# The delta rule's diagonal blocks, transposed and masked where they lie

## The chip, the cores and the metric

The kernel runs on one core of a Trainium2 chip. The metric is the device time of one execution in microseconds. The core has TensorE for matrix products, VectorE, ScalarE and GpSimd for elementwise work, and DMA queues for transfers. SBUF is the on-chip memory with 128 partitions; PSUM is where TensorE's products go.

## What is computed

One block of a network on a sequence of 512 rows of 2048 numbers, with three branches: a gated delta rule with 8 heads, an S5 state layer and a cross-attention to a memory. Their outputs are gated, summed and projected. The change lies in the delta rule. For each head and chunk it solves a triangular system, `eye + lower`:

```
def chunked_gated_delta_rule(q, k, v, g, beta):
    ...
    lower = jnp.where(strict, jnp.einsum('bnhid,bnhjd->bnhij', k_beta, k) * decay, 0.0)
    eye = jnp.eye(CHUNK, dtype=q.dtype)
    rhs = jnp.concatenate([v * beta[..., None], k_beta * jnp.exp(gc)[..., None]], axis=-1)
    sol = lax.linalg.triangular_solve(eye + lower, rhs, left_side=True, lower=True, unit_diagonal=True)
    u_val, w_dec = sol[..., :dv], sol[..., dv:]
    ...
```

## The kernel before

All large projections are written as products of float32 numbers split in a high and a low part: ScalarE makes `wh` of a weight block (line 508), VectorE makes `wl`, the rest (line 516), and TensorE runs three products for each pair of tiles (lines 522 to 524). A weight block comes in two halves of 128x1024, with two slots of each tile, and TensorE waits on semaphore `w_lo` before each half.

In the mixer stage the projections for head i+1 run on TensorE while the delta rule and the S5 groups of head i are worked on by the other engines. There are ten weight blocks per head, of eight portions each; the small products of the delta rule and of S5 are put between the portions. The order is written out by hand, for TensorE in one `mixer` function and for VectorE in another: each engine has one queue and goes through it in order, with semaphores between the engines.

The kernel takes chunks of 128 rows, four per head, so `NT` is 4 and `P` is 128. `system` (line 2378) writes the strictly lower matrices of the four chunks into `dl`, 128 partitions by 4 x 128. Their inverse is built from blocks of `B` = 32. `first_blocks` (lines 2385 to 2397) prepares the diagonal blocks: it gathers the sixteen 32x32 blocks into the tile `lb`, with one copy for each quarter of the partitions, transposes them into `lbt`, masks them with `low1` (first neighbours below the diagonal), subtracts the result from the identity in `tb`, and transposes that into `ub`. TensorE then works with `lbt`, `tb` and `ub` in `level_x` and `level_p` (lines 1176 to 1198). On VectorE, `first_blocks` stands behind `keys`, `system` and `values`, and in front of `split(3, 0)`, that is, of the `wl` half that TensorE needs next.

GpSimd has its own queue. In `turn_back` (lines 812 to 815) it multiplies S5's scanned states with cosines and sines, six products of 128x512 per group of states; in `arguments` (lines 791 to 802) it makes the arguments of the tables for a later group.

```
        if j: keys(j); system(j); values(j); first_blocks(j)
        split(3, 0)
        if j: queries(j)
        split(3, 1)
```

Of the kernel before, what the change touches and what calls it, by code (L numbers as in the profile page):

```python
# [21 lines left out]
ALU = mybir.AluOpType  # L22
# [3 lines left out]
P = 128  # L26
# [3 lines left out]
NT = S // P  # L30
# [16 lines left out]
B = 32  # L47
# [42 lines left out]
def count(j, first, per):  # L90

    return j[0] * per + (first + per * j[1])


def wait(e, s, value):

    if isinstance(value, int) and value <= 0:
        return
    e.wait_ge(s, value)


def wait_apart(k, e, s, value):


    wait(e, s, value)
    if not isinstance(value, int):
        e.sem_inc(k.sp_waits if e is k.sp else k.pool_waits if e is k.pool else k.pe_waits, 1)
# [6 lines left out]
def build(nc, x, mem, norm_g, w_in, conv_w, a_log, dt_bias, gdn_g, lam_re, lam_im, log_dt, b_re, b_im,  # L114
          c_re, c_im, s5_d, w_glu, mem_g, w_kv, w_a, w_b, w_c, w_out, final_g, consts, out):
    with ExitStack() as ctx:
        k = Handles()
# [16 lines left out]
        def sb(where, name, shape, dt=F32):  # L134
            return where.enter_context(nc.sbuf_tensor(name, [P] + shape, dt))
# [68 lines left out]
        with ExitStack() as area:  # L204
            k.qraw = sb(area, "qraw", [S + 3])
            k.kraw = sb(area, "kraw", [S + 3])
            k.vraw = sb(area, "vraw", [S + 3])
            k.qc = sb(area, "qc", [S])
            k.kc = sb(area, "kc", [S])
            k.vc = sb(area, "vc", [S])  # L210
            k.zs = sb(area, "zs", [S])
            k.zbs = sb(area, "zbs", [S])
            k.cwh = sb(area, "cwh", [CONV, 3])
            k.braw = sb(area, "braw", [2, 4, GS])
            k.craw = sb(area, "craw", [2, NS])
            k.bpad = sb(area, "bpad", [2, 4, 4, 2, GS])
            k.rq = sb(area, "rq", [S])
            k.zk = sb(area, "zk", [S])
            k.er = sb(area, "er", [NT, P])
            k.qd = sb(area, "qd", [NT, P])  # L220
            k.dl = sb(area, "dl", [NT, P])
            k.du = sb(area, "du", [NT, P])
            k.vb = sb(area, "vb", [NT, P])
            k.kbg = sb(area, "kbg", [NT, P])
            k.kd = sb(area, "kd", [NT, P])
            with ExitStack() as a:
                k.lt = sb(a, "lt", [NT, P])
                k.tl = sb(a, "tl", [NT, P])
            k.sql = sb(area, "sql", [NT, P], F32R)
            k.sqh = sb(area, "sqh", [NT, P], F32R)  # L230
            k.tu = sb(area, "tu", [NT, P])
            k.gx = sb(area, "gx", [NT, P])
            k.lb = sb(area, "lb", [NT, B])
            k.lbt = sb(area, "lbt", [NT, B])
            k.tb = sb(area, "tb", [NT, B])
            k.ub = sb(area, "ub", [NT, B])
            k.xb5 = sb(area, "xb5", [NT, B])
            k.th = sb(area, "th", [NT, 2 * B])
            k.vn = sb(area, "vn", [NT, P])
            k.st = sb(area, "st", [P])  # L240
            k.hph = sb(area, "hph", [4, NT])
            k.hk = sb(area, "hk", [4, NT])
            k.s5h = sb(area, "s5h", [5, 4])
            k.dh = sb(area, "dh", [1])
            k.xb = sb(area, "xb", [S])
            k.bt = sb(area, "bt", [4, 4, GS])
            k.cpad = sb(area, "cpad", [2, 2, NS])
            k.bs = sb(area, "bs", [2, 4, P], F32R)
            k.bc = sb(area, "bc", [2, P])
            k.tcos0 = sb(area, "tcos0", [S])  # L250
            k.tcos1 = sb(area, "tcos1", [S])
            k.tsin0 = sb(area, "tsin0", [S])
            k.tsin1 = sb(area, "tsin1", [S])
            k.karg = sb(area, "karg", [S])
            k.farg = sb(area, "farg", [S])
            k.onesr = sb(area, "onesr", [P], F32R)
            k.ma = sb(area, "ma", [S])
            k.mb = sb(area, "mb", [S])
            k.gr = [sb(area, f"gr{q}", [S]) for q in range(4)]
            with ExitStack() as a:  # L260
                k.gi0 = sb(a, "gi0", [S])
                k.gi1 = sb(a, "gi1", [S])
                k.hr = [sb(a, f"hr{q}", [S]) for q in range(4)]
            with ExitStack() as a:
                k.xbh = sb(a, "xbh", [S], F32R)
                k.xbl = sb(a, "xbl", [S], F32R)
                k.x4 = sb(a, "x4", [4, S], F32R)
# [722 lines left out]
def tensor_program(k, pe):  # L990
# [185 lines left out]
    def level_x(j, l):  # L1176

        if l == 1:
            wait_apart(k, pe, k.tu_s, count(j, 7, 8))
            wait_apart(k, pe, k.qkt, count(j, 1, 1))  # L1180
        else:
            wait_apart(k, pe, k.tus, count(j, 2 * l - 3, 17))
        for n in range(NT):
            for r in range(0, P, B):
                mm = pe.matmul(ps[2][r:r + B, n * B:(n + 1) * B], k.lbt[r:r + B, n, :], k.tb[r:r + B, n, :], start=True, stop=True)  # L1185
        mm.then_inc(k.lx, 1)

    def level_p(j, l):

        wait_apart(k, pe, k.xm, count(j, l, 7))  # L1190
        if l == 1:
            wait_apart(k, pe, k.tu_s, count(j, 8, 8))
        else:
            wait_apart(k, pe, k.tus, count(j, 2 * (l - 1), 17))
        for n in range(NT):
            for r in range(0, P, B):
                mm = pe.matmul(ps[6][r:r + B, n * B:(n + 1) * B], k.ub[r:r + B, n, :], k.xb5[r:r + B, n, :], start=True, stop=True)  # L1197
        mm.then_inc(k.lp, 1)
# [108 lines left out]
    def mixer(a, j, l, blocks=PER):  # L1307
# [46 lines left out]
        if j: level_x(j, 1)  # L1354
        until(39)
        if j: level_p(j, 1)
        until(43)
        if j: level_x(j, 2)
# [3 lines left out]
        if j: level_p(j, 2)  # L1362
        until(49)
        if j: level_x(j, 3)
        until(53)
        if j: level_p(j, 3)
# [653 lines left out]
def vector_program(k, dve):  # L2020
    ps, mat, blk, col, stat, tp, hp = k.ps, k.mat, k.blk, k.col, k.stat, k.tp, k.hp
# [8 lines left out]
    tt, ts, stt = dve.tensor_tensor, dve.tensor_scalar, dve.scalar_tensor_tensor  # L2030
# [235 lines left out]
    def rep_chunks(m, n=P):  # L2266
        return m.unsqueeze(1).to_broadcast([P, NT, n])
# [117 lines left out]
    def first_blocks(j):  # L2385

        dve.wait_ge(k.lm, count(j, 1, 1))
        wait(dve, k.lx, count(j, 0, 6))
        for r in range(0, P, B):
            dve.tensor_copy(k.lb[r:r + B, :, :], k.dl[r:r + B, :, r:r + B]).then_inc(k.tu_s, 1)  # L2390
        dve.wait_ge(k.tu_s, count(j, 4, 8))
        dve.transpose(k.lbt[:, :, :], k.lb[:, :, :]).then_inc(k.tu_s, 1)
        tt(k.tb[:, :, :], k.lb[:, :, :], rep_chunks(blk["low1"], B), ALU.mult).then_inc(k.tu_s, 1)
        dve.wait_ge(k.tu_s, count(j, 6, 8))
        tt(k.tb[:, :, :], rep_chunks(blk["ident"], B), k.tb[:, :, :], ALU.subtract).then_inc(k.tu_s, 1)
        dve.wait_ge(k.tu_s, count(j, 7, 8))
        dve.transpose(k.ub[:, :, :], k.tb[:, :, :]).then_inc(k.tu_s, 1)

    def blocked(bank, m=B):
# [94 lines left out]
    def mixer(a, j, l, blocks=PER, heads=True, x=None):  # L2494
# [23 lines left out]
        if j: keys(j); system(j); values(j); first_blocks(j)  # L2518
# [270 lines left out]
```

## Time and profile before

| | |
|---|---|
| median of 3 runs | 2090.88 us (2090.85 to 2091.57) |
| the profiled execution | 2091.08 us |
| its span, first to last instruction | 2089.3 us |
| TensorE busy | 2051.6 us, 98% |
| VectorE busy | 1347.7 us, 65% |
| ScalarE busy | 841.6 us, 40% |
| GpSimd busy | 844.8 us, 40% |

A row of the trace gives the start in us, the duration, the engine (PE is TensorE, DVE VectorE, ACT ScalarE, POOL GpSimd), the line of the kernel, the operation, what it writes and reads, and the shape. An engine's share of busy time alone doesn't tell what bounds the kernel; the waits of the busiest engine do.

### The profile page before, as it was taken

How to read it: one execution, taken by the hardware profiler on the slowest of the kernel's cores; microseconds unless marked ns; L12 is line 12 of the kernel's file. 1: busy time of each engine (PE TensorE's matmuls, PEld its weight loads, DVE VectorE, ACT ScalarE, POOL GpSimd, SP SyncE). 2: the span in 40 equal slices, each digit the busy share in tenths (PEclk: the TensorE clock that was granted, in tenths of full speed). 3: DMA queues.
4: the chain of work that ended last, by engine and by line, in shares of the span. 5: the costliest groups of instructions: out<-in, count | busy, mean ns of one | idle time of the engine just before them, and what ended most of it. 6: DMA issues, size and time to landing. Idle time of an engine off the chain costs nothing.

```text
span 2089.3 us, 32198 instructions
## 1 busy us (share of the span) xinstructions
PE 2051.6 (98%) x12700; PEld 1706.3 (82%) x12700; DVE 1347.7 (65%) x1831; ACT 841.6 (40%) x1113; POOL 844.8 (40%) x631
## 2 busy tenths in 40 slices
PE   7999999999999999999999999999999999999998
PEld 6799888887787877877778777777778888888997
DVE  6554353449789697796977969767443344557766
ACT  5433232354453444434444344363242232223444
POOL 0000000028577586774867848668201100024223
PEclk9999999999999999999999999999999999999999
DMA  9255453455554445555546546455456556455855
GB/s 279 81 156 151 137 171 91 116 131 116 119 123 120 129 113 125 144 133 129 152 126 153 133 126 155 119 144 124 116 161 197 172 153 184 145 147 188 264 174 182
DMA packets 416712, 306.88 MB, mean 147 GB/s; under 512 B 25817, under 2 KB 386626, under 8 KB 415938
## 3 DMA queue, kind: packets, MB, share of 16 engines
q1 hardware_dynamic: 394610, 236.73, 40.8%
q0 software_dynamic: 14736, 55.58, 10.9%
q10 hardware_dynamic: 7232, 12.72, 1.6%
q8 instruction: 92, 1.51, 0.3%
q14 instruction: 42, 0.34, 0.1%
HBM read 269.30 MB, written 60.83 MB: 158 GB/s over the span
## 4 chain that ended last, share of the span: by engine, by line
PE 80%; DVE 11%; ACT 4%; issue 3%; DMA 2%; POOLq 0%; POOL 0%; DVEq 0%; ACTq 0%; SPq 0%
PE bank L522 23%; PE bank L524 22%; PE bank L523 22%; PE bank L1480 2%; PE bank L1483 2%; PE bank L1484 2%; DVE lb L2390 2%; DVE wl L516 1%; DVE tl L2456 1%; DVE gi L2487 1%; PE bank L1304 1%; ACT wh L508 1%; PE bank L1185 1%; PE bank L1197 1%; DMA yst<-s_out 1%
## 5 line engine op out<-in xcount | busy, mean ns | idle before, releaser
L522 PE MATMUL bank<-uh,wh 128*128 128x512 f32 x2176 | 873.0, 401 | 9.4 <-DVE wl L516 6.5
L524 PE MATMUL bank<-uh,wl 128*128 128x512 f32 x2176 | 849.1, 390 | 0.0
L523 PE MATMUL bank<-ul,wh 128*128 128x512 f32 x2176 | 848.9, 390 | 0.0
L516 DVE TENSOR_TENSOR wl<-raw,wh 128x1024 fp32r<-128x1024 f32 x320 | 446.5, 1398 | 382.8 <-ACT wh L508 381.5
L508 ACT ACTIVATE wh<-raw 128x1024 fp32r<-128x1024 f32 x320 | 336.2, 1058 | 470.7 <-DMA raw<-in_w_in_dram 214.5
L522 PEld LDWEIGHTS bank<-uh,wh 128*128 128x128 f32 x2176 | 408.8, 188 | 102.7 <-issue 12.9
L524 PEld LDWEIGHTS bank<-uh,wl 128*128 128x128 f32 x2176 | 408.5, 188 | 88.3
L523 PEld LDWEIGHTS bank<-ul,wh 128*128 128x128 f32 x2176 | 409.2, 188 | 77.3
L771 POOL DMA_DIRECT2D gated_c<-ox x8 | 4.3, 544 | 372.4 <-DVE ox L2153 371.8
L812 POOL TENSOR_TENSOR hr<-tcos,gr 128x512 f32<-128x512 f32 x32 | 52.9, 1654 | 185.4 <-DVE gi L2487 185.4
L909 POOL DMA_DIRECT2D gates<-gates x24 | 17.1, 714 | 199.6 <-DVE merged L2682 127.8
L1702 ACT ACTIVATE gk<-bank 128x512 f32<-128x512 f32 x48 | 28.7, 597 | 164.2 <-PE bank L524 164.2
L522 PE MATMUL bank<-mh,wh 128*128 128x256 f32 x256 | 73.4, 287 | 5.5 <-DVE wl L516 5.5
L524 PE MATMUL bank<-mh,wl 128*128 128x256 f32 x256 | 72.3, 282 | 0.0
L523 PE MATMUL bank<-ml,wh 128*128 128x256 f32 x256 | 72.2, 282 | 0.0
L2615 DVE TENSOR_TENSOR wl<-raw,wh 128x1024 fp32r<-128x1024 f32 x32 | 47.8, 1495 | 31.7 <-ACT wh L1919 31.7
L1480 PE MATMUL bank<-wh,uh 128*128 128x256 f32 x240 | 67.5, 281 | 0.2 <-DVE ul L2598 0.2
L1484 PE MATMUL bank<-wh,ul 128*128 128x256 f32 x240 | 67.3, 281 | 0.0
L791 POOL TENSOR_SCALAR karg<-cst,s5h 128x512 f32<-128x512 f32 x32 | 24.4, 762 | 101.9 <-DVE hph L2274 90.7
L794 POOL TENSOR_SCALAR karg<-karg 128x512 f32<-128x512 f32 x32 | 62.9, 1964 | 0.0
L798 POOL TENSOR_SCALAR karg<-cst,s5h 128x512 f32<-128x512 f32 x32 | 61.3, 1915 | 3.2
L813 POOL TENSOR_TENSOR karg<-tsin,gi 128x512 f32<-128x512 f32 x32 | 62.0, 1938 | 0.0
(410 smaller groups left out, 3355.6 us busy)
## 6 DMA issues: line engine op xcount, KB each, us to landing
raw<-in_w_in_dram SPq DMA_DIRECT2D x224, 512.0 KB, 3.9
raw<-in_w_kv_mem_dram SPq DMA_DIRECT2D x32, 512.0 KB, 3.9
weight_sums<-in_w_out_dram POOLq DMA_DIRECT2D x32, 512.0 KB, 7.6
raw<-weight_sums SPq DMA_DIRECT2D x32, 512.0 KB, 3.8
gates<-gk ACTq DMA_DIRECT2D x48, 256.0 KB, 4.3
gates<-gates POOLq DMA_DIRECT2D x24, 512.0 KB, 4.5
weight_sums<-in_w_out_dram SPq DMA_DIRECT2D x16, 512.0 KB, 5.2
weight_sums<-weight_sums SPq DMA_DIRECT2D x16, 512.0 KB, 5.7
```

What stands on the lines that cost most here:

```text
L508: act.activation(k.wh[slot][:, c], k.raw[slot][:, c], ACT.Copy).then_inc(k.w_hi, 1)
L516: dve.tensor_tensor(k.wl[slot][:, c], k.raw[slot][:, c], k.wh[slot][:, c].bitcast(F32), ALU.subtract).then_inc(k.w_lo, 1)
L522: pe.matmul(o, ah, bh, start=start, stop=False)
L523: pe.matmul(o, ah, bl, start=False, stop=False)
L524: return pe.matmul(o, al, bh, start=False, stop=stop)
L794: ts(k.karg[:, :], k.karg[:, :], -ROUND, None, ALU.add).then_inc(k.args, 1)
L798: ts(k.karg[:, :], k.tvec, lo_, None, ALU.mult).then_inc(k.args, 1)
L812: pool.tensor_tensor(o[:, :], c1[:, :], a[:, :], ALU.mult).then_inc(k.dem, 1)
L813: pool.tensor_tensor(k.karg[:, :], c2[:, :], b[:, :], ALU.mult).then_inc(k.dem, 1)
L1480: mm = pe.matmul(o, hi[:, a], wh, start=t == 0 and i == 0, stop=False)
L1484: mm = pe.matmul(o, lo[:, a], wh, start=False, stop=t == KW - 1 and i == 1)
L2615: tt(k.wyl[n % 4], k.wyr[n % 4], k.wph[n % 2][:, Y_PART, :].bitcast(F32), ALU.subtract).then_inc(k.w_lo, 1)
```

## The change

The tile `lb` is gone. The mask reads the diagonal blocks in `dl` and writes `tb`, in four products of 32 partitions each; the transpose reads them in `dl` and writes `lbt`, in four of 32 partitions. The masks come first, the transposes behind them. The subtraction and the second transpose stay. Semaphore `tu_s` now counts 10 per head and not 8, and the waits on it follow, those of TensorE too.

```
@@ -1176,7 +1175,7 @@
         if l == 1:
-            wait_apart(k, pe, k.tu_s, count(j, 7, 8))
+            wait_apart(k, pe, k.tu_s, count(j, 9, 10))
             wait_apart(k, pe, k.qkt, count(j, 1, 1))
@@ -1189,7 +1188,7 @@
         if l == 1:
-            wait_apart(k, pe, k.tu_s, count(j, 8, 8))
+            wait_apart(k, pe, k.tu_s, count(j, 10, 10))
@@ -2387,13 +2386,12 @@
         dve.wait_ge(k.lm, count(j, 1, 1))
         wait(dve, k.lx, count(j, 0, 6))
         for r in range(0, P, B):
-            dve.tensor_copy(k.lb[r:r + B, :, :], k.dl[r:r + B, :, r:r + B]).then_inc(k.tu_s, 1)
-        dve.wait_ge(k.tu_s, count(j, 4, 8))
-        dve.transpose(k.lbt[:, :, :], k.lb[:, :, :]).then_inc(k.tu_s, 1)
-        tt(k.tb[:, :, :], k.lb[:, :, :], rep_chunks(blk["low1"], B), ALU.mult).then_inc(k.tu_s, 1)
-        dve.wait_ge(k.tu_s, count(j, 6, 8))
+            tt(k.tb[r:r + B, :, :], k.dl[r:r + B, :, r:r + B], rep_chunks(blk["low1"], B)[r:r + B], ALU.mult).then_inc(k.tu_s, 1)
+        for r in range(0, P, B):
+            dve.transpose(k.lbt[r:r + B, :, :], k.dl[r:r + B, :, r:r + B]).then_inc(k.tu_s, 1)
+        dve.wait_ge(k.tu_s, count(j, 4, 10))
         tt(k.tb[:, :, :], rep_chunks(blk["ident"], B), k.tb[:, :, :], ALU.subtract).then_inc(k.tu_s, 1)
-        dve.wait_ge(k.tu_s, count(j, 7, 8))
+        dve.wait_ge(k.tu_s, count(j, 9, 10))
         dve.transpose(k.ub[:, :, :], k.tb[:, :, :]).then_inc(k.tu_s, 1)
```

VectorE's queue in the first head, before, from the values `vb` to the next `wl`:

```order
L2363 TENSOR_TENSOR vb<-bank,hk 128x512
L2390 COPY lb<-dl 32x128 x4
L2392 STREAM_TRANSPOSE lbt<-lb 128x128
L2393 TENSOR_TENSOR tb<-lb,cst 128x128
L2395 TENSOR_TENSOR tb<-cst,tb 128x128
L2397 STREAM_TRANSPOSE ub<-tb 128x128
L516 TENSOR_TENSOR wl<-raw,wh 128x1024
```

And the same stretch of the changed kernel, whose line numbers are one or two lower:

```order
L2362 TENSOR_TENSOR vb<-bank,hk 128x512
L2389 TENSOR_TENSOR tb<-dl,cst 32x128 x4
L2391 STREAM_TRANSPOSE lbt<-dl 32x128 x4
L2393 TENSOR_TENSOR tb<-cst,tb 128x128
L2395 STREAM_TRANSPOSE ub<-tb 128x128
L515 TENSOR_TENSOR wl<-raw,wh 128x1024
```

Eight instructions became ten; what stands before and behind them, and every other engine's queue, is as it was.

## Rows read from the trace of the kernel before

**Rows 1.** The page, busy time of each engine, share of the span, instructions:
```profile
PE 2051.6 (98%) x12700; PEld 1706.3 (82%) x12700; DVE 1347.7 (65%) x1831; ACT 841.6 (40%) x1113; POOL 844.8 (40%) x631
```

**Rows 2.** The page, chain that ended last, share by engine and by line:
```profile
PE 80%; DVE 11%; ACT 4%; issue 3%; DMA 2%; POOLq 0%; POOL 0%; DVEq 0%; ACTq 0%; SPq 0%
PE bank L522 23%; PE bank L524 22%; PE bank L523 22%; PE bank L1480 2%; PE bank L1483 2%; PE bank L1484 2%; DVE lb L2390 2%; DVE wl L516 1%; DVE tl L2456 1%; DVE gi L2487 1%; PE bank L1304 1%; ACT wh L508 1%; PE bank L1185 1%; PE bank L1197
```

**Rows 3.** TensorE in order of time, first and last head, [idle before <-releaser]:
```profile
493.65 0.47 PE L522 MATMUL bank<-uh,wh 128*128 128x512 f32 x1 [0.25 <-DVE wl L516]
...
1417.46 0.47 PE L522 MATMUL bank<-uh,wh 128*128 128x512 f32 x1 [1.57 <-DVE wl L516]
```

**Rows 4.** VectorE in order of time, first head: start us, us, what:
```profile
485.81 0.71 DVE L2390 COPY lb<-dl 32x128 f32<-32x128 f32 x1
486.55 1.34 DVE L2390 COPY lb<-dl 32x128 f32<-32x128 f32 x1
487.92 1.20 DVE L2390 COPY lb<-dl 32x128 f32<-32x128 f32 x1
489.15 1.35 DVE L2390 COPY lb<-dl 32x128 f32<-32x128 f32 x1
490.54 0.31 DVE L2392 STREAM_TRANSPOSE lbt<-lb 128x128 f32<-128x128 f32 x1
490.77 0.58 DVE L2393 TENSOR_TENSOR tb<-lb,cst 128x128 f32<-128x128 f32 x1
491.39 0.67 DVE L2395 TENSOR_TENSOR tb<-cst,tb 128x128 f32<-128x128 f32 x1
492.09 0.32 DVE L2397 STREAM_TRANSPOSE ub<-tb 128x128 f32<-128x128 f32 x1
492.32 1.18 DVE L516 TENSOR_TENSOR wl<-raw,wh 128x1024 fp32r<-128x1024 f32 x1
```

**Rows 5.** GpSimd in order of time, same stretch:
```profile
485.15 1.29 POOL L815 TENSOR_TENSOR hr<-hr,karg 128x512 f32<-128x512 f32 x1
486.52 1.29 POOL L812 TENSOR_TENSOR gr<-tsin,gr 128x512 f32<-128x512 f32 x1
487.77 1.27 POOL L813 TENSOR_TENSOR karg<-tcos,gi 128x512 f32<-128x512 f32 x1
489.12 1.30 POOL L815 TENSOR_TENSOR gr<-gr,karg 128x512 f32<-128x512 f32 x1
490.52 0.69 POOL L791 TENSOR_SCALAR karg<-cst,s5h 128x512 f32<-128x512 f32 x1
491.20 1.59 POOL L792 TENSOR_SCALAR farg<-cst,s5h 128x512 f32<-128x512 f32 x1
```

**Rows 6.** VectorE's instructions by line, count: ns min/median/max, first and last start:
```profile
L2390 DVE COPY lb<-dl x32: 694/1270/1351, 485.8 to 1413.0; 32x128 f32<-32x128 f32 x32
L2416 DVE COPY th<-tb x16: 215/216/218, 542.1 to 1463.4; 32x128 f32<-32x128 f32 x16
L2404 DVE TENSOR_TENSOR xb<-bank,cst x32: 276/290/292, 503.5 to 1455.0; 128x128 f32<-128x128 f32 x32
```

**Rows 7.** The same view, small products with both inputs in SBUF:
```profile
L2360 DVE TENSOR_TENSOR hk<-hk,hph x8: 704/1350/1361, 484.4 to 1408.2; 128x4 f32<-128x4 f32 x8
L2355 DVE TENSOR_TENSOR hk<-hk,hph x8: 162/164/164, 460.4 to 1383.4; 128x4 f32<-128x4 f32 x8
L2292 DVE TENSOR_TENSOR bpad<-bt x32: 221/380/1315, 453.4 to 1372.8; 64x64 f32<-64x64 f32 x32
```

**Rows 8.** VectorE and GpSimd in order of time, near 454 us:
```profile
453.91 1.31 DVE L2292 TENSOR_TENSOR bpad<-bt 64x64 f32<-64x64 f32 x1
...
453.85 1.29 POOL L800 TENSOR_TENSOR farg<-farg,karg 128x512 f32<-128x512 f32 x1
```

**Rows 9.** Transposes of 32 partitions, by line, and four in order of time:
```profile
L2414 DVE STREAM_TRANSPOSE tu<-tb x32: 299/302/307, 540.7 to 1462.8; 32x128 f32<-32x128 f32 x32
...
540.72 1.30 DVE L2414 STREAM_TRANSPOSE tu<-tb 32x128 f32<-32x128 f32 x4
```

**Rows 10.** TensorE in order of time, first products on the diagonal blocks:
```profile
499.29 0.40 PE L1185 MATMUL bank<-tb,lbt 32*32 32x32 f32 x25
```

More of the change, by code:

```diff
@@ L232, in build @@
             k.gx = sb(area, "gx", [NT, P])
-            k.lb = sb(area, "lb", [NT, B])
             k.lbt = sb(area, "lbt", [NT, B])
```

## The prediction

> **What bounds the kernel now.** The profiled execution took 2091.08 us, 0.20 us more than the median of the runs shown, 2090.88; the sum is made on 2091.08 and then carried over to the median. The page's busy table comes first [rows 1]: TensorE is busy for 98% of the span. VectorE is at 65% and GpSimd at 40%. So the end is set by TensorE, and another engine counts only where TensorE waits for it. The chain that ended last [rows 2] gives 80% to TensorE and 11% to VectorE, and names the copies into `lb` (line 2390) with 2%. This invites the thought that the copies' whole time is on the path. The instructions with their idle times correct it: what TensorE stood still for is far smaller.
>
> TensorE's rows in order of time, with the idle time in front of each, have one wait per head at the place of the change, eight in all. The first is 0.25 us, the last 1.57 [rows 3]; the six between are 0.57 to 0.92, and the sum is 5.64 us. Each ends when the first `wl` (line 516) behind the diagonal blocks is there. In the first head VectorE's rows read [rows 4]: four copies 485.81 to 490.50, transpose, mask, subtraction, transpose, then `wl` 492.32 to 493.50; TensorE's next product starts at 493.65 [rows 3]. VectorE has no idle time in between. So whatever is added to or taken from these instructions moves that `wl`, and TensorE has no slack there, in any head. TensorE's next need of VectorE lies later in the same stretch and moves along with TensorE itself.
>
> **Why the copies are slow.** A copy of 32x128 elements between two SBUF tiles takes 215 ns at line 2416, yet these take 694 to 1351 ns [rows 6]. The rows of the four copies against those of GpSimd [rows 4, 5] show why: the copies end at 486.52, 487.89, 489.12 and 490.50, and GpSimd's operations end at 486.44, 487.81, 489.04 and 490.42. Each copy ends 0.08 us behind one of GpSimd's, and GpSimd's next one follows. The two engines take turns, and a copy pays for one GpSimd operation of 1.29 us, four in a row in each head.
>
> **The change part by part, per head.**
>
> 1. The four copies go, and four masked products of the same 32x128 elements take their place, each with two inputs in SBUF. Do they wait for their turn too? The trace has two kinds of small products with both inputs in SBUF to compare with. Line 2360 works on 4 elements per partition, among GpSimd's products, and takes 704 to 1361 ns, where line 2355, the same form elsewhere, takes 162 to 164. Line 2292 changes its first partition from one to the next as the new ones do, and goes from 221 to 1315 ns [rows 7]. One of these runs 453.91 to 455.22 and GpSimd's product 453.85 to 455.14 [rows 8], again a turn. So I take it that the four new products wait for the same four GpSimd operations. What differs is the part behind the wait: line 2393, such a product, ended at 491.35, 0.14 us behind the GpSimd operation that ended at 491.21 [rows 4, 5], the copies 0.08 behind. That is 0.06 us each, and GpSimd starts its next one that much later: 4 x 0.06 = +0.24 us. Bounds: 0, if the product is as quick as a copy, and 4 x 0.08 = 0.32, from the difference of the 292 ns that the product of line 2404 takes at most, on 128x128, and the 215 of line 2416 [rows 6].
>
> 2. The transpose of 128x128 becomes four of 32x128. Line 2414 is four such: 0.30 us each, 1.30 us for the four [rows 9], and with the gap of 0.03 us in front of the next instruction, as between the copies, 1.33. The one that goes took 0.23 us until the next started (490.54 to 490.77) [rows 4]. All 32 of line 2414 took 299 to 307 ns, so I take it that a transpose waits for no turn. That is +1.10 us; the lower bound is four steps of 0.23, +0.69.
>
> 3. The separate mask (line 2393) goes: 490.77 to the next start at 491.39 [rows 4], -0.62 us. It too had waited for a turn, behind GpSimd's operation of line 791.
>
> 4. The subtraction (line 2395) stays, but starts later. It took 0.67 us before, with the next start 0.70 us behind it; alone it should take what line 2404 takes on the same shape, 0.29 [rows 6]. I expect it to be free of a wait now: GpSimd's line 792 began at 491.20 [rows 5] and let the subtraction end at 492.06 [rows 4], so by taking off the product's 0.14 it gave way at 491.92, 0.57 us after the mask before it had ended. In the changed order the four products end at 490.74, GpSimd's two operations start at about 490.76 and 491.44, and the second gives way by 492.01. The subtraction starts at 490.77 + 1.33 = 492.10. So -0.38 us (0.32 with its gap for 0.70). If it must wait as before, this term is 0.
>
> The semaphore waits go from three to two and add nothing: what they wait for is a step earlier on the same engine. The first matmuls on `lbt` and `tb` start at 499.29 us, 7 us behind [rows 10], so their later start costs nothing; that cover would be gone only if the blocks came 7 us late. What stands behind the products on VectorE is `wl` and then the queries' mask; what waits for GpSimd, 0.24 us later, are sine and cosine tables for a later group of S5 states.
>
> Sum: 0.24 + 1.10 - 0.62 - 0.38 = **+0.34 us per head**, on a wait that TensorE already has. Eight heads: +2.7 us. 2091.08 + 2.7 = 2093.8, and on the median **2093.6 us**, 0.13% more. The bounds of parts 1 and 2 give -0.31 per head at the low end (0 + 0.69 - 0.62 - 0.38), -2.5 us, and +0.42 at the high end, +3.4 us.
>
> What the notes say on part 1 differs from page to page. The Trainium skill, page "Advanced Engine Details and Errata", section "VectorE Performance Modes", names only the two-port ("2p") instructions as those that "interfere/block eachother" with GpSimd's; by that alone the new products would run free, which is the first rival. The page "SBUF — State Buffer", section "Who interferes with whom", adds that a `tensor_tensor` with both inputs in SBUF contends with GpSimd's reads; lines 2360 and 2292 bear that one out.
>
> **Rivals.**
>
> *Faster: the products take no turns.* Then four of them take 4 x 0.32 = 1.28 us in place of the 4.73 from 485.81 to 490.54, and the block ends some 3.4 us sooner. TensorE can't get back more than it waits: 5.64 us, so 2085.4, on the median 2085.2. Even one turn saved of the four (1.3 us less, against +0.34) would take away the wait in all heads but the last. For it: half of line 2292's products got through in 0.22 to 0.38 us [rows 7]. Against it: line 2360, the long ones of line 2292, and that GpSimd has four products of its own queued in exactly this stretch, with gaps of at most 0.08 us between them [rows 5]. Chance 0.09.
>
> *Slower: the subtraction meets GpSimd's next operation.* The place is line 2395 against line 792. If that operation doesn't give way by 492.10, the time from which this decides, the subtraction takes its 0.67 us again, part 4 is 0, and the block is 0.24 + 1.10 - 0.62 = 0.72 us longer: 8 x 0.72 = +5.8, 2096.9, on the median 2096.7. For it: my margin is 0.09 us, and starts on GpSimd are roughly known. Against it: GpSimd and VectorE are shifted together, so that the margin hangs only on the transposes. Chance 0.13.
>
> *Slower still: the subtraction waits for the whole of line 792's record*, 1.59 us, to 491.44 + 1.58 = 493.02. It would end at 493.16, not 492.39: +0.34 + 0.77 = 1.11 us, eight times 8.9, on the median 2099.8. Against it: the subtraction before ended 0.73 us inside that record, and `wl` started inside it at 492.32 and took its usual 1.18 us [rows 4, 5]. Chance 0.03. The Trainium skill, "SBUF — State Buffer", section "SBUF: two separate sides", has the pair held "for the whole instruction", from which this case follows; the trace doesn't agree with it for this operation, at least by the recorded ends.
>
> **How the numbers follow.** The forecast, with its bounds 2088.4 to 2094.3, has 0.73, and within it most lies between +0.1 and +0.4 us per head, as the 299 ns of the transposes is measured and their 0.23 us step is not. The faster rival has 0.09, the slower ones 0.13 and 0.03, and 0.02 is left for what I don't see. The range is 2089.6 to 2097.0: it takes in the forecast but for the last of its lower bound, and the first slower rival, and leaves out about 0.16. A measurement of this kernel can tell about 0.2%, or 4.2 us, from no change: below 2086.7 is faster, above 2095.1 slower. The forecast lies within these. Faster 0.09, same 0.74, slower 0.17.
>
> **What would show it.** In the changed kernel four products of some 0.7 to 1.4 us stand where the copies stood, each ending about 0.14 us behind a GpSimd product. Four transposes of 0.30 us follow, and a subtraction of 0.29 us. TensorE's eight waits at this place grow from 5.6 us to about 8.4. I am wrong on part 1 if the products take 0.3 us and those waits vanish; on part 4 if the subtraction still shows 0.67 us.

## The result, and the profile after

The changed kernel takes 2094.22 us and the kernel before, run beside it, 2091.31 (medians of 22 runs each). The ratio is 1.0014, with a 95% interval from 1.0009 to 1.002: 2.9 us slower, between 1.9 and 4.2. The forecast was 2093.6, a change below the 0.2% that the prediction took for the least that a measurement can tell, and both hold. The measurement turned out finer than 0.2%: with 22 runs of each, 0.14% is told from nothing. The two profiled executions, from which all rows come, took 2093.31 and 2091.08 us.

VectorE in the first head of the changed kernel, in order of time (start in us, duration in us, engine, line, operation); it answers to [rows 4]:

```profile
485.33 0.77 DVE L2389 TENSOR_TENSOR tb<-dl,cst 32x128 f32<-32x128 f32 x1
486.13 1.34 DVE L2389 TENSOR_TENSOR tb<-dl,cst 32x128 f32<-32x128 f32 x1
487.50 1.26 DVE L2389 TENSOR_TENSOR tb<-dl,cst 32x128 f32<-32x128 f32 x1
488.79 1.35 DVE L2389 TENSOR_TENSOR tb<-dl,cst 32x128 f32<-32x128 f32 x1
490.17 1.31 DVE L2391 STREAM_TRANSPOSE lbt<-dl 32x128 f32<-32x128 f32 x4
491.50 0.29 DVE L2393 TENSOR_TENSOR tb<-cst,tb 128x128 f32<-128x128 f32 x1
491.83 0.31 DVE L2395 STREAM_TRANSPOSE ub<-tb 128x128 f32<-128x128 f32 x1
492.07 1.18 DVE L515 TENSOR_TENSOR wl<-raw,wh 128x1024 fp32r<-128x1024 f32 x1
```

GpSimd in the same stretch, against [rows 5]:

```profile
484.67 1.29 POOL L814 TENSOR_TENSOR hr<-hr,karg 128x512 f32<-128x512 f32 x1
486.03 1.29 POOL L811 TENSOR_TENSOR gr<-tsin,gr 128x512 f32<-128x512 f32 x1
487.28 1.33 POOL L812 TENSOR_TENSOR karg<-tcos,gi 128x512 f32<-128x512 f32 x1
488.69 1.30 POOL L814 TENSOR_TENSOR gr<-gr,karg 128x512 f32<-128x512 f32 x1
490.09 0.69 POOL L790 TENSOR_SCALAR karg<-cst,s5h 128x512 f32<-128x512 f32 x1
490.77 1.56 POOL L791 TENSOR_SCALAR farg<-cst,s5h 128x512 f32<-128x512 f32 x1
```

The masked products end at 486.10, 487.47, 488.76 and 490.14, GpSimd's at 485.96, 487.32, 488.61 and 489.99: each product ends 0.14 or 0.15 us behind one of GpSimd's. The copies ended 0.08 behind. From the first instruction of the block to the `wl` it is 492.07 - 485.33 = 6.74 us, where it was 492.32 - 485.81 = 6.51. So the block is 0.23 us longer; over the eight heads it is 0.22 to 0.24.

TensorE's rows at this place, first and last head, with the idle time in front; they answer to [rows 3]:

```profile
493.40 0.47 PE L521 MATMUL bank<-uh,wh 128*128 128x512 f32 x1 [0.58 <-DVE wl L515]
...
1418.99 0.47 PE L521 MATMUL bank<-uh,wh 128*128 128x512 f32 x1 [1.79 <-DVE wl L515]
```

The eight waits are 0.58, 0.83, 0.84, 0.84, 0.82, 1.12, 0.84 and 1.79 us, 7.66 in sum, against 5.64 before. They didn't all grow by the same: in each trace one of the middle waits is 0.3 us longer than its neighbours, before it is the fourth (0.92), after the sixth (1.12), and so the fourth shrank by 0.08 and the sixth grew by 0.52. From one head's `vb` to the next it is 131.75 us between the second and third head, where it was 131.51 (748.23 - 616.48 and 748.26 - 616.75).

```profile
748.23 0.69 DVE L2362 TENSOR_TENSOR vb<-bank,hk 128x512 f32<-128x512 f32 x1
```

The page of the changed kernel has TensorE busy for 98% still, and VectorE's busy time 0.3 us lower than in [rows 1] (1347.7). That isn't the block, in which VectorE is busy for 1.2 us more over the eight heads; the `wl` instructions of lines 516 and 515 took 1.7 us less in sum (446.5 and 444.8).

```profile
PE 2052.9 (98%) x12700; PEld 1708.4 (82%) x12700; DVE 1347.4 (64%) x1847; ACT 841.5 (40%) x1113; POOL 847.1 (40%) x631
```

### The profile page after: what moved, and what is told of

It is laid out like the page before. It is cut to its first block, busy times and chain, and to the rows that moved or that the text cites. A ratio compares the mean times of both kernels' runs of the same rounds, so it can differ in the third digit from the quotient of the medians.

```text
span 2091.6 us, 32214 instructions
## 1 busy us (share of the span) xinstructions
PE 2052.9 (98%) x12700; PEld 1708.4 (82%) x12700; DVE 1347.4 (64%) x1847; ACT 841.5 (40%) x1113; POOL 847.1 (40%) x631
## 4 chain that ended last, share of the span: by engine, by line
PE 81%; DVE 11%; ACT 3%; issue 3%; DMA 1%; POOL 0%; DVEq 0%; ACTq 0%; SPq 0%
PE bank L521 24%; PE bank L523 23%; PE bank L522 23%; PE bank L1479 2%; PE bank L1482 2%; PE bank L1483 2%; DVE tb L2389 2%; DVE wl L515 1%; DVE tl L2454 1%; DVE gi L2485 1%; PE bank L1303 1%; ACT wh L507 1%; PE bank L1184 1%; PE bank L1196 1%; DVE ma L2478 1%
## 5 line engine op out<-in xcount | busy, mean ns | idle before, releaser
L515 DVE TENSOR_TENSOR wl<-raw,wh 128x1024 fp32r<-128x1024 f32 x320 | 444.8, 1392 | 384.3 <-ACT wh L507 382.8
```

Source lines behind the costliest of these rows:

```text
L515: dve.tensor_tensor(k.wl[slot][:, c], k.raw[slot][:, c], k.wh[slot][:, c].bitcast(F32), ALU.subtract).then_inc(k.w_lo, 1)
```

## The experiments

Nine kernels were run, each timed beside the kernel before. They ask three things: whether time at this place reaches the end, whether the products and copies are slow because they take turns with GpSimd, and what is left when the turns are gone. The edits are shown by the instructions that they add, take out or move; the counts in the semaphore waits that follow from them are left out in part.

### Does time at this place reach the end? Transposes twice

```
+        for r in range(0, P, B):
+            dve.transpose(k.lb[r:r + B, :, :], k.dl[r:r + B, :, r:r + B]).then_inc(k.tu_s, 1)
```

> The changed kernel with four more transposes of the same blocks, into a scratch tile, right behind the first four. It asks whether time added to VectorE in this place reaches the end one to one. Theory (TensorE waits here in every head, with no slack): four transposes step by 1.33 us in the changed kernel's trace (1.31 and a gap), so each head grows by 1.33 us and the run by 8 x 1.33 = 10.6 us over the changed kernel, about 13 us over the kernel before (ratio 1.0062); TensorE's eight waits at this place grow from 7.7 us to about 18.3. Rival (part of it is absorbed, or more than it comes out because everything behind shifts against GpSimd and the DMA): less than 8 or more than 13 us over the changed kernel.

Measured: 2106.74 us, ratio 1.0071 (1.0057 to 1.0085), 12.5 us over the changed kernel where 10.6 was foretold. In the trace five of the seven distances between heads are 133.10 to 133.12 us, 1.34 more than the 131.76 or so of the changed kernel. That is the four transposes, 1.33 us, one to one. The last, which is longer in every kernel, is 135.99 against 134.68. One is left, 134.71, from the second head to the third, and in it are 1.6 us that the transposes don't explain. There, TensorE's wait in the second head was of the same length as in the third to seventh (2.15 us against 2.16 or 2.17), but its clock fell behind it. These are the rows of stretches of 4 us: length, busy us (instructions) of TensorE, its weight loads, VectorE, ScalarE and GpSimd, the granted clock as a share, and DMA:

```profile
625.00:629.00 4.00, 1.85 (x7) 1.22 (x6) 3.84 (x9) 1.65 (x2) 3.86 (x3) 0.88 0.45 97
629.00:633.00 4.00, 4.00 (x14) 3.19 (x13) 3.89 (x5) 2.83 (x3) 3.78 (x3) 0.69 0.28 100
```

14 products in 4 us where 17 or more fit at full clock (one per 0.23 us): a granted 0.69 is a mean of 2.4 and 1.2 GHz over the stretch. The same came behind the 3.12 us wait of the last head (0.65 and 0.50 in its two stretches). The theory holds for the block (one to one), and the surplus in the trace is TensorE's clock falling behind a wait, in one head of six with equal waits.

### The turns. Transposes in front of the products

```
+        for r in range(0, P, B):
+            dve.transpose(k.lbt[r:r + B, :, :], k.dl[r:r + B, :, r:r + B]).then_inc(k.tu_s, 1)
         for r in range(0, P, B):
             tt(k.tb[r:r + B, :, :], k.dl[r:r + B, :, r:r + B], rep_chunks(blk["low1"], B)[r:r + B], ALU.mult).then_inc(k.tu_s, 1)
-        for r in range(0, P, B):
-            dve.transpose(k.lbt[r:r + B, :, :], k.dl[r:r + B, :, r:r + B]).then_inc(k.tu_s, 1)
-        dve.wait_ge(k.tu_s, count(j, 4, 10))
+        dve.wait_ge(k.tu_s, count(j, 8, 10))
```

> The changed kernel with the four transposes in front of the four masked products; the same instructions in another order. Theory (turns with GpSimd's products, a transpose takes none): the transposes run while GpSimd is in its products and use 1.33 us of what was waiting; then only three full turns are left for the products and the fourth meets GpSimd's short operation of line 790 (0.69 us), so that one takes about 0.7 us and not 1.35, and the subtraction meets the next one and takes 0.6 to 0.7 us again, not 0.29. Sum per head about 0.2 us less than the changed kernel, -1.6 us, so within 0.1% of the kernel before. Rival (a masked product has a price of its own of about 1.3 us, whatever GpSimd does): the products still take 1.2 us on average, the subtraction 0.29, and the time is that of the changed kernel, +2.9 us over before.

Measured: 2092.25 us, ratio 1.0007 (0.9998 to 1.0016). VectorE in the second head:

```profile
617.89 1.29 DVE L2389 STREAM_TRANSPOSE lbt<-dl 32x128 f32<-32x128 f32 x4
...
619.22 0.82 DVE L2391 TENSOR_TENSOR tb<-dl,cst 32x128 f32<-32x128 f32 x1
620.07 1.26 DVE L2391 TENSOR_TENSOR tb<-dl,cst 32x128 f32<-32x128 f32 x1
621.36 1.34 DVE L2391 TENSOR_TENSOR tb<-dl,cst 32x128 f32<-32x128 f32 x1
622.73 0.76 DVE L2391 TENSOR_TENSOR tb<-dl,cst 32x128 f32<-32x128 f32 x1
...
623.52 0.67 DVE L2393 TENSOR_TENSOR tb<-cst,tb 128x128 f32<-128x128 f32 x1
```

The fourth product met GpSimd's short operation and took 0.76 us, and the subtraction took 0.67 again, as foretold. The block is 6.57 us, 0.17 less than in the changed kernel (0.2 expected). The same instructions have other durations in another order, so a product has no price of its own of 1.3 us. The transposes took 1.29 us for the four while GpSimd was in its products: they take no turn. One row must be read with care: for most heads the trace names ScalarE's `gk` as what ended TensorE's wait here, but TensorE starts 0.15 us behind the end of `wl` as in every other kernel (625.79 against 624.46 + 1.18 = 625.64).

### The other terms without the products. Copies and four transposes

```
         for r in range(0, P, B):
             dve.tensor_copy(k.lb[r:r + B, :, :], k.dl[r:r + B, :, r:r + B]).then_inc(k.tu_s, 1)
-        dve.wait_ge(k.tu_s, count(j, 4, 8))
-        dve.transpose(k.lbt[:, :, :], k.lb[:, :, :]).then_inc(k.tu_s, 1)
+        for r in range(0, P, B):
+            dve.transpose(k.lbt[r:r + B, :, :], k.dl[r:r + B, :, r:r + B]).then_inc(k.tu_s, 1)
```

> The kernel before with only the transpose changed: the four copies stay and feed the mask, the transpose reads the blocks in place, in four of 32 partitions, behind the copies. It measures parts 2 to 4 of the sum without part 1. Theory: copies 4.73 us as before, transposes 1.33, mask and subtraction behind them both free of a turn, 0.32 each with gap, second transpose 0.24: 6.94 us from the first copy to the next wl where the kernel before has 6.51, +0.43 per head, +3.4 us, ratio 1.0016. Rival (mask and subtraction wait for a turn here too, 0.6 to 0.7 each): +1.1 per head, +8.6 us.

Measured: 2098.26 us, ratio 1.0034 (1.0021 to 1.0048), twice what was expected. The block is what it should be, but the `wl` behind it isn't. The second head:

```profile
617.73 4.70 DVE L2390 COPY lb<-dl 32x128 f32<-32x128 f32 x4
622.46 1.30 DVE L2392 STREAM_TRANSPOSE lbt<-dl 32x128 f32<-32x128 f32 x4
623.79 0.29 DVE L2394 TENSOR_TENSOR tb<-lb,cst 128x128 f32<-128x128 f32 x1
624.12 0.29 DVE L2396 TENSOR_TENSOR tb<-cst,tb 128x128 f32<-128x128 f32 x1
624.45 0.31 DVE L2398 STREAM_TRANSPOSE ub<-tb 128x128 f32<-128x128 f32 x1
624.68 1.67 DVE L516 TENSOR_TENSOR wl<-raw,wh 128x1024 fp32r<-128x1024 f32 x1
...
624.67 1.50 POOL L794 TENSOR_SCALAR karg<-karg 128x512 f32<-128x512 f32 x1
```

From the first copy to `wl` it is 624.68 - 617.73 = 6.95 us, computed 6.94, and mask and subtraction are both free of a turn. But GpSimd's line 794 starts at 624.67, 0.01 us ahead of `wl`, and `wl` takes 1.67 us, not 1.18. In the first, fourth and fifth heads the two starts are as close (889.60 and 889.61 in the fourth), but there `wl` got in first and took 1.18 us, and GpSimd's operation 2.56. The distance to the next head is 132.0 us there, 0.4 or 0.5 more than before; from the second, third and sixth head it is 132.5. Five `wl` that lose 0.49 us are 2.5 us, which with the 3.4 foretold makes 5.9. TensorE's eight waits grew by as much, from 5.64 to 11.59 us. The last 1 us of the 6.9 measured isn't explained. The changed kernel's `wl` starts at 492.07 in the first head and GpSimd's operation at 492.31, so it kept 0.24 us of distance from this. The mechanism is the turn again, at an instruction that I hadn't looked at.

### Shorter turns. GpSimd's products in halves

```
-                pool.tensor_tensor(o[:, :], c1[:, :], a[:, :], ALU.mult).then_inc(k.dem, 1)
-                pool.tensor_tensor(k.karg[:, :], c2[:, :], b[:, :], ALU.mult).then_inc(k.dem, 1)
-                wait_apart(k, pool, k.dem, n + 2)
-                pool.tensor_tensor(o[:, :], o[:, :], k.karg[:, :], op).then_inc(k.dem, 1)
+                for w in (slice(0, S // 2), slice(S // 2, S)):
+                    pool.tensor_tensor(o[:, w], c1[:, w], a[:, w], ALU.mult).then_inc(k.dem, 1)
+                for w in (slice(0, S // 2), slice(S // 2, S)):
+                    pool.tensor_tensor(k.karg[:, w], c2[:, w], b[:, w], ALU.mult).then_inc(k.dem, 1)
+                wait_apart(k, pool, k.dem, n + 4)
+                for w in (slice(0, S // 2), slice(S // 2, S)):
+                    pool.tensor_tensor(o[:, w], o[:, w], k.karg[:, w], op).then_inc(k.dem, 1)
```

> The changed kernel with GpSimd's products of 128x512 in turning the S5 states back cut in two of 128x256 each. The work is the same, a turn is half as long. Theory (a masked product waits for one GpSimd operation): each takes about 0.75 us and not 1.3, the block is some 2 us shorter, and TensorE's waits at this place (7.7 us in sum, 1.8 at most) vanish: about 7 us less than the changed kernel, ratio to before about 0.998. Rival (the products are slow by themselves): they stay at 1.3 us, and the time stays or grows, as GpSimd has 192 more operations to start.

Measured: 2084.15 us, ratio 0.9965 (0.9951 to 0.9978). The masked products by line (count: ns min/median/max, first and last start), and GpSimd's:

```profile
L2392 DVE TENSOR_TENSOR tb<-dl,cst x32: 268/716/787, 484.9 to 1405.0; 32x128 f32<-32x128 f32 x32
...
L817 POOL TENSOR_TENSOR gr<-gr,karg x64: 722/739/1727, 489.6 to 1485.3; 128x256 f32<-128x256 f32 x64
```

VectorE's instructions are those of the changed kernel, in the same order, and its products went from a median of 1296 ns to 716. That settles that their time is GpSimd's. The first product of each head, 268 to 271 ns, met no turn. The Trainium skill, page "SBUF — State Buffer", section "Who interferes with whom", says that a VectorE instruction with two SBUF inputs contends with a GpSimd instruction that reads SBUF. The trace agrees: 268 against 716 and 1296 ns. The block fell from 6.74 to 4.5 or 5.0 us, as foretold, and the waits at this place are gone. The time fell by 10.1 us against the changed kernel, not by about 7: the recorded waits understate what TensorE loses, as the next experiment shows.

### No copies and no products. The gather by transposes

```
         for r in range(0, P, B):
-            dve.tensor_copy(k.lb[r:r + B, :, :], k.dl[r:r + B, :, r:r + B]).then_inc(k.tu_s, 1)
+            dve.transpose(k.lbt[r:r + B, :, :], k.dl[r:r + B, :, r:r + B]).then_inc(k.tu_s, 1)
         dve.wait_ge(k.tu_s, count(j, 4, 8))
-        dve.transpose(k.lbt[:, :, :], k.lb[:, :, :]).then_inc(k.tu_s, 1)
+        dve.transpose(k.lb[:, :, :], k.lbt[:, :, :]).then_inc(k.tu_s, 1)
+        dve.wait_ge(k.tu_s, count(j, 5, 8))
```

> The kernel before with the copies taken out: four transposes of 32 partitions read the blocks in place and write the transposed tile, one transpose of 128x128 turns that back into the gathered tile, and mask, subtraction and last transpose are as before. Theory (transposes take no turn, so all four turns of the copies are saved): transposes 1.33 us and 0.34, mask and subtraction wait for one GpSimd product each (about 0.7 and 1.4 us), and the wl behind them for another, so it is there some 1.9 us sooner than before; TensorE's waits at this place vanish, and the time is 5.6 us less than before, ratio 0.9973. This is also the size of the faster rival of the prediction. Rival (TensorE then waits a little later for the same engine): less than 3 us gained.

Measured: 2083.79 us, ratio 0.9962 (0.9949 to 0.9976), 8.0 us less than before, where 5.6 was foretold. No version found is faster than this one by more than the noise. VectorE in the second head:

```profile
616.92 1.29 DVE L2390 STREAM_TRANSPOSE lbt<-dl 32x128 f32<-32x128 f32 x4
618.25 0.31 DVE L2392 STREAM_TRANSPOSE lb<-lbt 128x128 f32<-128x128 f32 x1
618.60 0.47 DVE L2394 TENSOR_TENSOR tb<-lb,cst 128x128 f32<-128x128 f32 x1
619.10 1.26 DVE L2396 TENSOR_TENSOR tb<-cst,tb 128x128 f32<-128x128 f32 x1
620.39 0.31 DVE L2398 STREAM_TRANSPOSE ub<-tb 128x128 f32<-128x128 f32 x1
620.63 2.04 DVE L516 TENSOR_TENSOR wl<-raw,wh 128x1024 fp32r<-128x1024 f32 x1
```

The block is 3.71 us instead of 6.51. `wl` now pays for a turn itself, 2.04 us, and is still done 1.9 us sooner after the start of the block. TensorE's wait at this place is gone, and the third head follows the second by 130.68 us, 0.83 less than before.

The gain is more than the 5.64 us of recorded idle time that I took for the most that can be had. In [rows 3] the first wait is 0.25 us; but TensorE's last product before it starts at 493.01 and the next at 493.65, where products without a wait follow by 0.23:

```profile
493.01 0.39 PE L524 MATMUL bank<-uh,wl 128*128 128x512 f32 x1
```

That is 0.41 us lost for 0.25 us shown, since a product's row lasts 0.39 us and overlaps the next one. So 0.16 us are hidden in front of the product. Behind it another 0.08 are, since the next one follows by 0.31 us and not 0.23:

```profile
493.96 0.40 PE L523 MATMUL bank<-ul,wh 128*128 128x512 f32 x1
```

With 0.24 us per head the eight waits cost 5.64 + 8 x 0.24 = 7.6 us. TensorE has the same 12700 products in both traces, so they can be compared product by product: from in front of the first wait to behind the eighth the version without copies gains 7.6 us. The profiled executions differ by 7.3 us (2083.79 and 2091.08), the medians by 8.0.

### The wl half first, with the old block and with the new

```
-        if j: keys(j); system(j); values(j); first_blocks(j)
+        if j: keys(j); system(j); values(j)
         split(3, 0)
+        if j: first_blocks(j)
```

> The kernel before with the one wl half taken in front of the diagonal blocks; the blocks as they were. Theory: the blocks are needed only some 7 us later, so TensorE's waits at this place vanish: 5.6 us less than before, ratio 0.9973. Rival (VectorE is too full in this stretch, the next wl or the queries come late instead): less than 3 us gained.

> The changed kernel with the same wl half in front of the diagonal blocks. Theory (the change costs its 0.24 us per head only through that wl): the same time as the kernel before with this order, to within 0.5 us, so the change is worth nothing there. Rival (the change costs also somewhere else, such as by shifting GpSimd, or in the 1 us that the measured difference of 2.9 us has over 8 x 0.24): it stays slower by 1 to 3 us.

Measured: 2089.82 us with the old block, ratio 0.9992 (0.9983 to 1.0001), and 2095.27 with the new one, 1.0014 (1.0005 to 1.0023). Both expectations fell: 2.0 us were gained where 5.6 were foretold, and the new block costs more in this order, not nothing. The waits at `wl` vanish, but others come in their place a little later, at the first level's second product, which waits for VectorE's `xb` (first row of each kernel's second head):

```profile
635.28 0.45 PE L1197 MATMUL bank<-xb,ub 32*32 32x32 f32 x32 [0.84 <-DVE xb L2404]
```

```profile
636.27 0.45 PE L1196 MATMUL bank<-xb,ub 32*32 32x32 f32 x32 [1.44 <-DVE xb L2402]
```

VectorE's queue has no gap from the block to that `xb`. The 7 us of cover that the prediction named for the blocks was read off the first matmul that uses them, and it isn't there for what stands behind them in VectorE's queue: making the blocks wait makes the whole queue late.

And in this order the change costs more, 5.5 us by the medians, and not nothing or 1 to 3 us. The fourth copy in the second head of the one, and the fourth product in the other:

```profile
622.65 0.25 DVE L2390 COPY lb<-dl 32x128 f32<-32x128 f32 x1
```

```profile
623.15 0.76 DVE L2389 TENSOR_TENSOR tb<-dl,cst 32x128 f32<-32x128 f32 x1
```

GpSimd's short operation starts at 622.64 and 623.07. The copy, 0.01 us behind it, got through in 0.25 us; the product, 0.08 us behind, waited for its end. It is the same in all eight heads (0.25 and 0.76 us). So one turn of four depends on some hundredths of a microsecond, and 0.5 us per head with it. The heads follow one another by 0.6 us more on the average, 4.2 us over the seven distances; one head of the profiled execution has 1.7 us more, from TensorE's clock.

### Two cures at once

The `wl` half first and the gather by transposes together:

> Both together: the wl half first and the gather by transposes. Theory (after either of them no wait is left at this place): no more than either alone, ratio 0.997 to 0.9975. Rival (VectorE's load in the whole stretch sets something else too): up to 3 us less than either.

Measured: 2083.84 us, ratio 0.9963 (0.9949 to 0.9977).

The gather by transposes and GpSimd's products in halves together:

> The gather by transposes and GpSimd's products in halves in one kernel. With each alone the heads follow one another by 130.7 us in the trace, 0.8 less than before, and no wait of TensorE is left at this place. Theory (130.7 us is TensorE's own time for a head, so a second cure has nothing to take): the time of the gather by transposes alone, ratio 0.996 to 0.9965. Rival (VectorE's other waits for GpSimd still cost): below 0.995.

Measured: 2083.75 us, ratio 0.9964 (0.9950 to 0.9977). Neither is faster than one cure alone, and in all four kernels with a cure the heads follow one another by 130.3 to 131.1 us, but for the first and the last distance, and mostly by 130.7. What TensorE loses at this place is all that was to be had, and one cure takes it.

## Why the prediction held, step by step

- **The bound.** That TensorE has no slack at this `wl` in any head held: the transposes put in twice came out one to one, 1.34 us for 1.33.
- **Part 1, the products take the copies' turns.** The mechanism held: the ends 0.14 to 0.15 us behind GpSimd's were forecast at 0.14, and halving GpSimd's operations cut the products from 1296 to 716 ns. The size was off: +0.24 us was forecast, and the block's four steps grew from 4.73 to 4.84 us (485.33 to 490.17), +0.11. The step that failed is "and GpSimd starts its next one that much later", four times. From one start to the next, GpSimd took 1.37, 1.25, 1.35 and 1.40 us before and 1.36, 1.25, 1.41 and 1.40 after. Only the third grew, by 0.06, and in the other heads by 0.04 or 0.05. Of the four GpSimd operations that follow a product, three stand behind a pause of their own of 0.07 to 0.10 us; I take it that this covers the longer product, though no run tests it apart. The one without such a pause (line 813 before, 812 after) is the one whose row grew, from 1.27 to 1.33 us. The rest of the 0.11 is the tail of the last product.
- **Part 2, the transposes.** +1.10 forecast, 1.33 - 0.23 measured (490.17 to 491.50). They ran beside GpSimd's operations at 299 to 309 ns in all 32.
- **Part 3, the mask gone.** -0.62, as read from before.
- **Part 4, the subtraction free of its turn.** 0.29 us in all eight heads, with the gap 0.33, so -0.37 where -0.38 was forecast. The margin of 0.09 us held and was wider, since GpSimd wasn't held up four times: by the prediction's own reckoning its line 791 gave way by 490.77 + 0.57 = 491.34, 0.16 us before the subtraction started.
- **The sum.** +0.11 + 1.10 - 0.62 - 0.37 = +0.22, and the traces show 0.22 to 0.24 per head, where 0.34 was forecast: eight heads are 1.9 us of VectorE's time, not 2.7. The waits grew to 7.66 us, not 8.4.
- **Why 2.9 us all the same.** Product by product, TensorE in the changed kernel is 0.6 us ahead in front of the first wait at this place, where no changed instruction has run yet, and 1.5 us late behind the eighth (1418.99 against 1417.46). That is 2.1 us in eight heads, where the recorded waits grew by 2.0 (7.66 - 5.64). Behind the last head TensorE's clock fell in the changed kernel after a wait of 2.56 us for ScalarE, and not before after one of 2.67. The rows for 1536 to 1538 us are, after and before (columns as above):

```profile
1536.00:1538.00 2.00, 1.46 (x4) 1.21 (x5) 1.53 (x2) 1.54 (x3) 0.02 (x1) 0.50 0.99 262
```

```profile
1536.00:1538.00 2.00, 2.00 (x11) 1.65 (x10) 1.33 (x2) 1.87 (x2) 0.00 (x0) 1.00 0.78 197
```

  A granted 0.50 is 1.2 GHz. Six products took 2.70 us in place of 1.44 (1536.54 to 1539.24, and 1535.11 to 1536.55). It looks like the rest of the difference and isn't: soon after, TensorE stands still in the kernel before, and doesn't in the changed one, where the same product starts at 1554.38 with no idle time in front:

```profile
1552.50 0.50 PE L522 MATMUL bank<-uh,wh 128*128 128x512 f32 x1 [0.82 <-DVE wl L516]
```

  In both traces the product starts 0.06 us behind the end of that `wl` (1552.44 and 1554.32), so without the clock's fall it would have started no sooner. The `wl` stands in VectorE's queue behind instructions that wait for ScalarE's work on S5's output, and the first of ScalarE's rows there are as far apart, 1.88 us, before and after:

```profile
1544.92 0.63 ACT L1864 ACTIVATE yst<-yst 128x512 f32<-128x512 f32 x1 [7.03 <-DMA yst<-s_out]
```

```profile
1546.80 0.63 ACT L1863 ACTIVATE yst<-yst 128x512 f32<-128x512 f32 x1 [7.48 <-DMA yst<-s_out]
```

  Their load was issued in front of the clock's fall, 1.43 us later than before (1534.55 against 1533.12), and took 12.2 us and not 11.8. So in this trace it is the slower load that came through to the end, and the clock's time did not. Another 0.5 us came behind TensorE's last product. The two spans differ by -0.6 + 2.1 + 0.3 + 0.5 = 2.3 us (2091.6 and 2089.3), of which 2.1 is the change. What makes the medians differ by 2.9 stays open; 2.1 lies within the interval, near its edge. That the sum of 2.7 came nearer to the medians than the 2.1 of the traces is not to its credit.
- **The rivals.** None came in. The size of the faster one was mis-read: TensorE can get back 7 to 8 us here and not 5.64, as the gather by transposes showed. The step behind it, "TensorE can't get back more than it waits", took the recorded idle time for all that is lost. The slower one, the subtraction meeting a turn, is real in another order: with the transposes in front it took 0.67 us.

## What to carry to other kernels

In this kernel small VectorE instructions that copy between SBUF tiles or read two of them paid for a whole GpSimd operation each (1.2 to 1.35 us), where GpSimd had a row of its own; only the first, which came in the middle of one, paid less. Count the instructions that take a turn, not their elements, and try a form that takes none (here a transpose and a transpose back, 1.68 us where the copies and their transpose took 4.96) or cut GpSimd's operations in two. To replace one such form by another changed next to nothing (4.84 us for 4.73). And read the cost of an edit up to the next instruction that takes a turn: a few hundredths of a microsecond decided about 0.5 us at two places here. Last, the idle time that a trace shows in front of TensorE's products is less than what is lost: compare starts.

## What the runs showed of the hardware

- A transpose on VectorE took 299 to 309 ns for 32x128 in all 32 instances of the changed kernel, beside GpSimd's work, 0.30 us for a quarter of the partitions where all 128 took 0.31. The Trainium skill, page "SBUF — State Buffer", section "Who interferes with whom", has instructions with at most one SBUF input outside the two-port modes free of GpSimd; these rows agree.
- Whether a VectorE instruction that asks just behind the start of a GpSimd operation gets in first isn't fixed: 0.01 us behind, a copy got in (0.25 us); 0.08 behind, a product didn't (0.76); and a `wl` 0.01 behind lost 0.49 us in five heads and won in three.
- TensorE's clock can fall to 1.2 GHz (a granted 0.50) behind a wait of about 2 us and need not: after 2.15 us it did in one head, after 2.16 or 2.17 in five others it didn't; in the `wl`-first version of the changed kernel it fell in the sixth head, where TensorE had waited 1.76 us, and from it to the next head it took 1.7 us longer than elsewhere. Nor need the time come through: in the changed kernel six products behind a fall lost 1.3 us, and none of it reached the end.
